# Per-token inverse rms, earlier key norms, paired low-rank products and moved second-half inputs in a hybrid decoder layer

## The chip, the cores and the metric

The kernel runs on one core of a Trainium2 chip. The metric is the device time of one execution in microseconds (us); lower is better. TensorE's granted clock is given as a share of full speed: 1.00 is 2.4 GHz, 0.50 is 1.2 GHz.

## The reference

One decoder layer on 512 tokens of width 1024, in float32:

```python
xn = x * rsqrt(mean(x*x) + 1e-6) * g_mix
z = xn @ w_in                          # 14 column tiles of 128 for RWKV, 8 for q and k, 512 columns of v
# RWKV-7 time mixing, 8 heads of 64, on z's first part (mixed with the previous token by mu)
decay = exp(-exp(-softplus(-(w0 + tanh(wd) @ w_up)) - 0.5))
a = sigmoid(a0 + ad @ a_up);  g = sigmoid(gd) @ g_up      # ranks 64, 64, 128
kk = k*k_k / max(norm_per_head(k*k_k), 1e-12);  k = k*(1 + (a-1)*k_a)
state = state*decay + (state @ -kk) (kk*a)^T + v k^T;  y = state @ r     # token by token
# dilated sliding-window attention, 8 heads of 64, rope on q and k
h = x + concat(groupnorm(y)+bonus, gated by g; attention) @ w_out
out = rms_norm(h + peer_ffn(rms_norm(h)))                 # product-key experts
```

## The kernel before

The program is a row of stages, and each engine runs its own written-out list of instructions; semaphores order them. The order is the order of the code. A stage ends for all engines together. The stages that the change touches take the first 330 us of 1735: `project`, `attend`, `prepare` and `scan`. The later ones (`finish`, `route`, `experts`) are not touched.

**`project`** multiplies x by w_in in 26 steps n. The operands are split in a high and a low part (`xn_hi`, `xn_lo`, `win_hi`, `win_lo`, type fp32r), and each product is three matmuls (`three_pass`, L203 to L205). Step n needs `win_hi` (ScalarE, L288) and `win_lo` (VectorE, L354). The normalization is applied afterwards: VectorE multiplies each result by `rstd`, the inverse rms of every token, spread over 128 partitions by 512 tokens (`take`, L323). ScalarE squares x (`sq`, in tile `qk`), TensorE sums the squares with a matrix of ones in the middle of step 1 (`squares`, L383), VectorE scales and takes the reciprocal (L307, L309), ScalarE the root (L294). VectorE's list then has `take(0)`, `take(1)` and only then `win_lo` of step 3. Before step 4, TensorE transposes `rstd` (L394) so that `x_rstd_col` has one token per partition; ScalarE uses it at the end for the four tiles of v (L299). At the start `NWARM` matmuls on zeros run while the first inputs load.

**`attend`** runs over i = 0 to 15 (4 head pairs by 4 query tiles). TensorE's list has `scores(i)` (L492, two 64-row matmuls for two heads), `turn(i-3)` (transposes, L501), `values` (L513, L528); VectorE takes the row maxima (L637) and scales (L650), ScalarE exponentiates (L587) and copies the turned tiles out (`take`, L596). At i = 16 TensorE sums the squares of the keys per head (`square_sums`, L547, 16 matmuls of 8 columns), and at i = 18 ScalarE takes the root of them (L619), which needs another function table.

**`prepare`** makes the inputs of the recurrence. Twelve low-rank products of 512 columns (`up`, L723: 0 to 3 decay, 4 to 7 a, 8 to 11 gate) and four that spread the inverse key norms (`spread`, L730) run on TensorE in the order 0-3, two spreads, 4-7, two spreads, 8-11. ScalarE takes the sigmoids in the order of the products (L751), VectorE the running sums (L780), `k_new` (L794), the normed keys (L784), and then the scaled inputs of the first half of the tokens (`scaled_half`, L672 to L688, in steps 0 to 5).

**`scan`** handles 8 chunks of 64 tokens, four per half. For chunks 0 to 3 TensorE multiplies the scaled inputs (all its matmuls here have line L933), VectorE masks the results (`take_b`, `take_k`, L1129). Then the triangular matrices are inverted in five levels (`inverses`, L1150, L1156). After each level of the first half VectorE does steps of `scaled_half` for the second half of the tokens, step 3 after the last. The chain over chunks (`chain`) starts when all of these (semaphore `s_late`) are done; GpSimd then multiplies `bonus` by `k_new` (L920).

## Time and profile before

| what | value |
|---|---|
| median of 3 runs | 1736.76 us (1733.96 to 1739.7) |
| the profiled execution | 1737.52 us, its span 1735.4 us |
| mean granted clock of TensorE | 0.983 |
| busy: PE, DVE, ACT, POOL | 1672.4, 1330.6, 700.9, 610.7 us |

PE is TensorE's matmuls, PEld its weight loads, DVE VectorE, ACT ScalarE, POOL GpSimd. Times in the profile count from the start of the span; the 2.1 us between time and span lie around it.
### The profile page before, as it was taken

Reading aid. Unit: us, or ns where it says so; the run is one execution under the profiler, and the core shown is the slowest. Engines: PE = TensorE matmul, PEld = TensorE weight load, DVE = VectorE, ACT = ScalarE, POOL = GpSimd, SP = SyncE. Lnnn points to the kernel's source line nnn. Section 1 sums busy time; section 2 is a strip of 40 time slices with the busy share of each in tenths; the row PEclk is TensorE's granted clock in tenths of the full one; section 3 lists DMA queues with packets and bytes.
Section 4 is the critical chain, followed back from the end, with each engine's and each line's share of the span. In section 5 each row is a group of like instructions: output and inputs, shape, how many; then the busy total and the mean of one; then the engine's idle time right before and its main releaser. Section 6 shows DMA issues by size and latency. Waiting matters only on the chain.

```text
span 1735.4 us, 29171 instructions
## 1 busy us (share of the span) xinstructions
PE 1672.4 (96%) x11401; PEld 1475.1 (85%) x11401; DVE 1330.6 (77%) x2732; ACT 700.9 (40%) x1080; POOL 610.7 (35%) x393
## 2 busy tenths in 40 slices
PE   9999989989899999999999999999999999999997
PEld 6877459968788888999999999999999998778886
DVE  5654755567399998999936668888888888888777
ACT  4111752224333334888853333333333333333334
POOL 0000110100256675333342236556565555443120
PEclk9999899999999999999999999999999999999999
DMA  6220010012223344455779788999999999999994
GB/s 237 87 96 25 1 50 4 4 55 105 79 97 116 116 150 156 164 215 204 269 270 343 242 288 323 366 348 349 349 351 359 355 335 323 396 371 365 326 313 177
DMA packets 128040, 380.88 MB, mean 219 GB/s; under 512 B 12064, under 2 KB 52384, under 8 KB 126880
## 3 DMA queue, kind: packets, MB, share of 16 engines
q1 hardware_dynamic: 81104, 207.28, 33.6%
q0 software_dynamic: 37728, 159.40, 24.8%
q10 hardware_dynamic: 9072, 12.35, 2.0%
q8 instruction: 90, 1.47, 0.3%
q14 instruction: 46, 0.38, 0.1%
HBM read 339.92 MB, written 39.06 MB: 218 GB/s over the span
## 4 chain that ended last, share of the span: by engine, by line
PE 46%; DVE 10%; DMA 2%; ACT 0%; issue 0%; POOL 0%; SPq 0%; DVEq 0%; ACTq 0%; POOLq 0%
PE ps L203 15%; PE ps L205 15%; PE ps L204 15%; DVE gated_cols L2116 5%; DVE wout_raw L2116 2%; DMA mixed<-hidden_ahead 2%; DVE wout_raw L2119 2%; PE ps L2234 1%; DVE v_lo L2169 0%; DVE h L2191 0%; ACT v_hi L2080 0%; DVE h L2198 0%; POOL u_lo L1976 0%; ACT u_selected L2041 0%; SPq L1924 0%
## 5 line engine op out<-in xcount | busy, mean ns | idle before, releaser
L203 PE MATMUL ps<-v_hi,a_hi 128*128 128x512 f32 x768 | 300.0, 391 | 4.6 <-DVE a_lo L2172 4.4
L204 PE MATMUL ps<-v_lo,a_hi 128*128 128x512 f32 x768 | 299.5, 390 | 0.0
L205 PE MATMUL ps<-v_hi,a_lo 128*128 128x512 f32 x768 | 299.5, 390 | 0.0
L1993 POOL DMA_INDIRECT v_selected<-in_v,expert_index x128 | 184.4, 1440 | 295.6 <-DVE h L2139 281.7
L203 PE MATMUL ps<-xn_hi,u_hi 128*128 128x384 f32 (+1 forms) x800 | 275.0, 344 | 10.6 <-DMA sub_keys<-in_keys_t 5.1
L204 PE MATMUL ps<-xn_lo,u_hi 128*128 128x384 f32 (+1 forms) x800 | 272.2, 340 | 0.0
L205 PE MATMUL ps<-xn_hi,u_lo 128*128 128x384 f32 (+1 forms) x800 | 272.1, 340 | 0.0
L2169 DVE TENSOR_TENSOR v_lo<-wout_raw,v_hi 128x1024 fp32r<-128x1024 f32 x128 | 156.7, 1224 | 100.6 <-ACT v_hi L2080 99.3
L1984 POOL DMA_INDIRECT u_selected<-in_u_rows,expert_index x128 | 180.2, 1407 | 138.7 <-DVE hidden_selected L2126 109.0
L2080 ACT ACTIVATE v_hi<-wout_raw 128x1024 fp32r<-128x1024 f32 x128 | 135.0, 1054 | 139.3 <-PE ps L205 139.3
L2073 ACT ACTIVATE hidden<-ps 128x384 f32<-128x384 f32 x68 | 33.4, 491 | 358.8 <-PE ps L205 358.8
L203 PEld LDWEIGHTS ps<-v_hi,a_hi 128*128 128x128 f32 x768 | 144.5, 188 | 35.0 <-DVE v_lo L2169 6.0
L205 PEld LDWEIGHTS ps<-v_hi,a_lo 128*128 128x128 f32 x768 | 144.6, 188 | 30.0
L1586 POOL TENSOR_TENSOR wq_lo<-wq_raw,wq_hi 128x1024 fp32r<-128x1024 f32 x44 | 113.0, 2569 | 157.8 <-ACT wq_hi L1633 157.8
L204 PEld LDWEIGHTS ps<-v_lo,a_hi 128*128 128x128 f32 x768 | 144.5, 188 | 27.3
L2139 DVE SCALAR_TENSOR_TENSOR h<-v_selected,act_selected,h 128x1024 f32<-128x1024 f32 x128 | 163.9, 1280 | 4.4 <-DMA v_selected<-in_v,expert_index 0.7
L203 PEld LDWEIGHTS ps<-xn_hi,u_hi 128*128 128x128 f32 x800 | 151.4, 189 | 15.0 <-DMA sub_keys<-in_keys_t 5.4
L2126 DVE CUSTOM_DVE_ANT_0 dot_products<-u_selected,xn_tok 128x1024 bf16<-128x1024 f32 x128 | 153.6, 1219 | 13.4 <-DMA u_selected<-in_u_rows,expert_index 13.3
L204 PEld LDWEIGHTS ps<-xn_lo,u_hi 128*128 128x128 f32 x800 | 151.4, 189 | 2.9
L205 PEld LDWEIGHTS ps<-xn_hi,u_lo 128*128 128x128 f32 x800 | 151.2, 189 | 0.6
L203 PE MATMUL ps<-xn_hi,wq_hi 128*128 128x384 f32 (+1 forms) x352 | 128.0, 364 | 6.6 <-POOL wq_lo L1586 6.5
L205 PE MATMUL ps<-xn_hi,wq_lo 128*128 128x384 f32 (+1 forms) x352 | 125.5, 356 | 0.0
(319 smaller groups left out, 3116.5 us busy)
## 6 DMA issues: line engine op xcount, KB each, us to landing
wq_raw<-in_u_t SPq DMA_DIRECT2D x128, 512.0 KB, 4.8
wout_raw<-in_v SPq DMA_DIRECT2D x128, 512.0 KB, 7.0
gate_matrix<-gate_stage POOLq DMA_DIRECT2D x6, 4096.0 KB, 14.3
gates<-gate_matrix SPq DMA_DIRECT2D x32, 768.0 KB, 8.2
win_raw<-in_win_t SPq DMA_DIRECT2D x25, 512.0 KB, 3.5
mixed<-hidden_ahead SPq DMA_DIRECT2D x60, 192.0 KB, 7.4
wq_raw<-in_wq_t SPq DMA_DIRECT2D x16, 512.0 KB, 3.9
hidden_ahead<-hidden_route ACTq DMA_DIRECT2D x30, 192.0 KB, 2.0
```

Source lines behind the costliest of these rows:

```text
L203: nc.tensor.matmul(out, w_hi, m_hi, start=first, stop=False)
L204: nc.tensor.matmul(out, w_hi, m_lo, start=False, stop=False)
L205: return nc.tensor.matmul(out, w_lo, m_hi, start=False, stop=last)
L1586: st.do(pool.tensor_tensor(w_lo[:, n % SPL, :], raw[:, n % RQ, :], w_hi[:, n % SPL, :].bitcast(F32), ALU.subtract), s_lo)
L1984: pool.indirect_dma_start(u_sel[:, i % GB, :], None, u_rows, bass.IndirectOffsetOnAxis(S.expert[:, i:i + 1], 0)).then_inc(s_usel[i % GB], 16)
L1993: pool.indirect_dma_start(v_sel[:, k % GB, :], None, v_rows, bass.IndirectOffsetOnAxis(S.expert[:, k:k + 1], 0)).then_inc(s_vsel[k % GB], 16)
L2080: act.activation(v_hi[:, n % 2, :], v_raw[:, n % VR, :], ACT.Copy).then_inc(s_vhi, 1)
L2116: v.tensor_scalar(cols[r % R][:, q, :], S.const("iota"), tab[:, 1, tok:tok + 1], tab[:, 2, tok:tok + 1], ALU.is_equal, ALU.mult).then_inc( ...
L2119: v.tensor_tensor(rows[r % R][:, :, :], bc(S.const("iota"), 1, Q), bc(tab[:, 0, r * Q:(r + 1) * Q], 2, NKEY), ALU.is_equal).then_inc(s_row ...
L2126: v.tensor_tensor_reduce(products[:, i % 2, :], u_sel[:, i % GB, :], S.xn_tok[:, :], 1.0, 0.0, ALU.mult, ALU.add, h_sel[:, i:i + 1]).then_ ...
L2139: v.scalar_tensor_tensor(S.h[:, GT, :], v_sel[:, k % GB, :], a_sel[:, k:k + 1], S.h[:, GT, :], ALU.mult, ALU.add).then_inc(s_sum, 1)
L2169: v.tensor_tensor(v_lo[:, p, :], v_raw[:, n % VR, :], v_hi[:, p, :].bitcast(F32), ALU.subtract).then_inc(s_vlo, 1)
```

## The change

- `project`: the sums of squares come out with one token per partition: 32 matmuls (4 token tiles by 8 tiles of x) whose weights are a 128x128 tile of the squares and whose moving operand is one column of ones. Scaling, reciprocal and root work on 128x4. VectorE then multiplies the identity by each token's value (`tmp`, 4 times 128x128), TensorE spreads that over all partitions with ones in the middle of step 2 (`spread`), and VectorE copies the result to `rstd`. The transposes before step 4 are gone. The last step signals after each token tile, so that ScalarE takes v tile by tile. `NWARM` goes from 24 to 15.
- `attend`: `square_sums` moves to i = 8 (bank 7), VectorE copies the sums out at i = 10, ScalarE takes the root at i = 16, right after the tanh.
- `prepare`: decay and a products alternate and use only their 64 rows of the contraction each (partitions 0 to 63, and 64 to 127); the spreads follow, then the gate products. ScalarE alternates too. VectorE does all running sums, all `k_new`, all normed keys.
- `scan`: steps 0, 1, 3 and 5 for the second half stand after the masks of chunks 0 to 3, steps 4 and 2 after levels 0 and 1. Step 3 is one instruction in place of four.

```diff
-                st.do(v.tensor_scalar(rstd[:, :], S.ps[:, 3, :], 1.0 / D, RMS_EPS, ALU.mult, ALU.add), s_mean)
-                st.settle()
-                st.do(v.reciprocal(rstd[:, :], rstd[:, :]), s_mean)
+                st.do(v.tensor_scalar(rstd_col[:, :], S.ps[:, 3, 0:TT], 1.0 / D, RMS_EPS, ALU.mult, ALU.add))
+                st.settle()
+                st.do(v.reciprocal(rstd_col[:, :], rstd_col[:, :]), s_mean)
+                dve.wait_ge(s_const, 48)
                 dve.wait_ge(s_rstd, 1)
+                for t in range(TT):
+                    st.do(v.tensor_scalar(tmp[:, 0, t * P:(t + 1) * P], S.const("ident"), rstd_col[:, t:t + 1], None,
+                                          ALU.mult), s_col)
+                dve.wait_ge(s_spread, 1)
+                st.do(v.tensor_copy(rstd[:, :], S.ps[:, 7, :]))
+                st.settle()
...
             def squares():
                 pe.wait_ge(s_const, 48)
-                for k in range(KT):
-                    pe.wait_ge(s_sq, k + 1)
-                    last = nc.tensor.matmul(S.ps[:, 3, :], S.const("ones"), sq[:, k, :], start=k == 0,
-                                            stop=k == KT - 1)
+                pe.wait_ge(s_sq, KT)
+                for t in range(TT):
+                    for k in range(KT):
+                        last = nc.tensor.matmul(S.ps[:, 3, t:t + 1], sq[:, k, t * P:(t + 1) * P],
+                                                S.const("ones")[:, 0:1], start=k == 0, stop=k == KT - 1)
                 last.then_inc(s_ms, 1)
+            def spread():
+                pe.wait_ge(s_col, TT)
+                for t in range(TT):
+                    last = nc.tensor.matmul(S.ps[:, 7, t * P:(t + 1) * P], S.const("ones"),
+                                            tmp[:, 0, t * P:(t + 1) * P], start=True, stop=True)
+                last.then_inc(s_spread, 1)
...
+                        if n == 2 and k == KT // 2:
+                            spread()
...
+                        if n == NWIN - 1:
+                            last.then_inc(s_vmm, 1)
...
                 if i == 2 * TT:
                     pe.wait_ge(s_vt, 8)
                     pe.wait_ge(s_vta, 8)
-                if i == NS:
                     square_sums()
+                if i == 3 * TT:
+                    pe.wait_ge(s_sum, 1)
...
                 if i == NS:
                     st.do(act.activation(WA[0:HD, :], WA[0:HD, :], ACT.Tanh))
-                if i == NS + 2:
-                    act.wait_ge(s_ssum, 1)
-                    st.do(act.activation(nrm[:, :], S.ps[:, 0, 0:TT * NHD], ACT.Sqrt), s_nrm)
+                    act.wait_ge(s_sum, 1)
+                    st.do(act.activation(nrm[:, :], nrm[:, :], ACT.Sqrt), s_nrm)
...
+            for j in range(HP):
+                w = slice(j * P, (j + 1) * P)
+                nc.tensor.matmul(S.ps[:, j, :], S.up[0:HD, 0, w], WA[0:HD, :], start=True, stop=True).then_inc(s_up, 1)
+                nc.tensor.matmul(S.ps[:, HP + j, :], S.up[HD:P, 1, w], WA[HD:P, :], start=True,
                                  stop=True).then_inc(s_up, 1)
...
-        for j in range(HP):
-            st.do(v.tensor_tensor(r_[:, j, :, :], R[:, j, x].rearrange("p (n t) -> p n t", t=C), after[:, j, :, :],
-                                  ALU.mult), signal)
+        st.do(v.tensor_tensor(r_, R[:, :, x].rearrange("p j (n t) -> p j n t", t=C), after, ALU.mult), signal)
...
-                        if not half and c == HC - 1:
-                            st.settle()
-                            for step in ((0,), (1, 5), (4,), (2,), (3,))[level]:
-                                scaled_half(S, dve, v, st, step, 1, s_late)
+                        if not half and c == HC - 1 and level < 2:
+                            other_half((4, 2)[level])
...
             for ch in range(HC):
                 take_b(ch)
                 take_k(ch)
+                other_half((0, 1, 3, 5)[ch])
```

On ACT at the end of `attend`, before (`probs_t<-ps` is `take`, `mixed<-ps` is `pair`, `z_mixed<-z_mixed` the tanh):

```order
L596 ACTIVATE probs_t<-ps 128x8x128
L616 ACTIVATE z_mixed<-z_mixed 64x512
L596 ACTIVATE probs_t<-ps 128x2x3x128
L603 ACTIVATE mixed<-ps 128x512
L596 ACTIVATE probs_t<-ps 128x2x2x128
L619 ACT_TABLE_LOAD
L619 ACTIVATE kk_norm<-ps 128x32
L596 ACTIVATE probs_t<-ps 128x2x128
```

The same place after the change:

```order
L608 ACTIVATE probs_t<-ps 128x8x128
L628 ACTIVATE z_mixed<-z_mixed 64x512
L630 ACT_TABLE_LOAD
L630 ACTIVATE kk_norm<-kk_norm 128x32
L608 ACTIVATE probs_t<-ps 128x2x3x128
L615 ACTIVATE mixed<-ps 128x512
L608 ACTIVATE probs_t<-ps 128x2x2x128
L608 ACTIVATE probs_t<-ps 128x2x128
```

The table load and the root now stand ahead of `take(13)` and `pair(1)`, where they stood behind `take(14)`.

On DVE in `scan`, from the last level's masks of the first half to the first chunk of the chain, before:

```order
L677 SCALAR_TENSOR_TENSOR r_and_a<-kk,decays 128x4x63 x4
L679 TENSOR_SCALAR r_and_a<-kk 128x4x4
L1150 TENSOR_TENSOR level_products<-ps,consts_scan 128x4x32 x4
L1156 TENSOR_TENSOR inverse_t<-inverse_t,ps 128x4x32 x4
L682 TENSOR_TENSOR r_and_a<-z_mixed,decays 128x4x64 x4
L684 COPY chunk_decay<-decays 128x4x4
L1177 TENSOR_TENSOR b_scaled<-ps,v_products 128x256
```

The same place after the change:

```order
L1143 TENSOR_TENSOR level_products<-ps,consts_scan 128x4x32 x4
L1149 TENSOR_TENSOR inverse_t<-inverse_t,ps 128x4x32 x4
L1168 TENSOR_TENSOR b_scaled<-ps,v_products 128x256
L1169 TENSOR_TENSOR b_scaled<-z_mixed,v_products 128x256
L1118 TENSOR_TENSOR inverse_t<-ps,consts_scan 128x256
```

Steps 2 and 3 of the second half (L677 to L684) are gone from in front of the chain.

## Rows read from the trace of the kernel before

**Rows 1.** The page: each engine's busy time, share and instructions.

```profile
PE 1672.4 (96%) x11401; PEld 1475.1 (85%) x11401; DVE 1330.6 (77%) x2732; ACT 700.9 (40%) x1080; POOL 610.7 (35%) x393
```

**Rows 2.** Timeline of `project`'s head: start us, us, instruction, idle before and releaser.

```profile
18.51 7.09 PE L383 MATMUL ps<-qk,consts 128*128 128x512 f32 x16
...
25.04 0.80 PE L203 MATMUL ps<-xn_hi,win_hi 128*128 128x512 f32 x1
...
30.42 0.69 DVE L323 TENSOR_TENSOR z_shift<-ps,x_rstd 128x512 f32<-128x512 f32 x1 [0.70 <-ACT x_rstd L294]
...
36.12 0.50 PE L203 MATMUL ps<-xn_hi,win_hi 128*128 128x512 f32 x1 [2.31 <-DVE win_lo L354]
...
43.34 0.60 PE L394 MATMUL ps<-consts_late,x_rstd 128*128 128x128 f32 x4
```

**Rows 3.** Timeline, PE: the key sums at `attend`'s end, 16 matmuls.

```profile
216.45 3.74 PE L547 MATMUL ps<-to_head_scaled,kk_square 128*128 128x8 f32 x32
```

**Rows 4.** Stretches: busy us and count of PE, PEld, DVE, ACT, POOL; granted clock; DMA.

```profile
37.38:40.79 3.41, 3.41 (x9) 2.64 (x8) 2.10 (x3) 0.00 (x0) 0.00 (x0) 0.50 0.48 154
197.80:201.20 3.40, 3.40 (x14) 1.65 (x10) 1.22 (x8) 1.31 (x6) 0.00 (x0) 0.50 0.00 0
216.45:220.05 3.60, 3.60 (x35) 3.60 (x33) 1.57 (x7) 1.88 (x5) 0.00 (x0) 1.00 0.00 0
...
301.47:307.00 5.53, 5.53 (x76) 5.53 (x78) 4.24 (x5) 0.38 (x1) 4.71 (x2) 0.50 0.01 3
309.13:315.54 6.41, 6.41 (x198) 6.41 (x196) 3.78 (x11) 1.97 (x7) 0.73 (x1) 1.00 0.02 5
```

**Rows 5.** Timeline: `project`'s end and `attend`'s first matmuls.

```profile
170.72 2.42 ACT L299 ACTIVATE v_tok<-ps,x_rstd_col 128x512 f32<-128x512 f32 x4 [16.12 <-PE ps L205]
...
173.45 0.49 PE L492 MATMUL ps<-qk 64*128 64x128 f32 x4 [2.81 <-PEq L211]
```

**Rows 6.** Timeline, PE in `attend`: after `scores(8)`, and a pair of 512 columns.

```profile
196.67 0.63 PE L501 MATMUL ps<-consts_late,scores 128*128 128x128 f32 x4 [0.57 <-DVE scores L650]
...
204.47 1.13 PE L492 MATMUL ps<-qk 64*128 64x512 f32 x4
```

**Rows 7.** Timeline of `attend`'s tail, ACT and PE.

```profile
217.72 0.61 ACT L616 ACTIVATE z_mixed<-z_mixed 64x512 f32<-64x512 f32 x1
220.94 0.81 ACT L596 ACTIVATE probs_t<-ps 128x768 f32<-128x768 f32 x1 [2.61 <-PE ps L501]
221.65 0.59 ACT L603 ACTIVATE mixed<-ps 128x512 f32<-128x512 f32 x1
...
224.71 1.28 ACT L619 ACT_TABLE_LOAD   x1
...
222.38 1.09 PE L528 MATMUL ps<-probs_t,v_tok 128*64 128x128 f32 x16 [0.47 <-ACT mixed L603]
```

**Rows 8.** Timeline of `prepare`: PE's products, DVE's wait for the third spread, step 0.

```profile
234.42 3.70 PE L723 MATMUL ps<-z_mixed,up_weights 128*128 128x512 f32 x8
...
239.21 0.75 DVE L784 SCALAR_TENSOR_TENSOR kk<-z_mixed,params,ps 128x512 f32<-128x512 f32 x1 [2.00 <-PE ps L730]
...
242.02 1.23 DVE L672 TENSOR_TENSOR k_new<-k_new,z_mixed 128x1024 f32<-128x1024 f32 x1
```

**Rows 9.** Timeline of `scan`: DVE before chunk 3's masks, and the start of the chain.

```profile
265.20 0.42 DVE L1129 TENSOR_TENSOR inverse_t<-ps,consts_scan 128x256 f32<-128x256 f32 x1 [2.45 <-PE ps L933]
...
299.49 0.29 DVE L1156 TENSOR_TENSOR inverse_t<-inverse_t,ps 128x128 f32<-128x128 f32 x1 [0.18 <-PE ps L933]
299.81 1.43 DVE L682 TENSOR_TENSOR r_and_a<-z_mixed,decays 128x256 f32<-128x256 f32 x4
...
301.41 4.52 POOL L920 TENSOR_TENSOR z_mixed<-z_mixed,k_new 128x2048 f32<-128x2048 f32 x1 [34.98 <-DVE chunk_decay L684]
...
301.47 0.80 PE L933 MATMUL ps<-z_mixed,r_and_a 64*64 64x64 f32 x10 [2.04 <-DVE chunk_decay L684]
...
303.07 3.13 DVE L1178 TENSOR_TENSOR b_scaled<-z_mixed,v_products 128x256 f32<-128x256 f32 x1
```

More of the change, by code:

```diff
@@ L390, in _ @@
             for n in range(NWIN):
-                if n == SPL + 1:
-                    pe.wait_ge(s_rstd, 1)
-                    for t in range(TT):
-                        last = nc.tensor.transpose(S.ps[:, 7, t * P:(t + 1) * P], rstd[:, t * P:(t + 1) * P],
-                                                   S.const("ident"))
-                    last.then_inc(s_col, 1)
                 pe.wait_ge(*((s_lo, n + 1) if n else (s_lo_half, 1)))
@@ L418, in _ @@
                                               w_hi[:, n % SPL, w], w_lo[:, n % SPL, w], k == 0, k == KT - 1)
-                last.then_inc(s_mm, 1)
+                        if n == NWIN - 1:
+                            last.then_inc(s_vmm, 1)
+                if n < NWIN - 1:
+                    last.then_inc(s_mm, 1)
                 if NRW < n < NRW + NQK + 1:
@@ L543, in square_sums @@
                 pe.wait_ge(s_ksq, 2 * HP)
-                pe.wait_ge(s_bias, 2 * NS)
                 for q in range(TT):
                     for j in range(HP):
-                        last = nc.tensor.matmul(S.ps[:, 0, q * NHD:(q + 1) * NHD], ksq[:, j, q * P:(q + 1) * P],
+                        last = nc.tensor.matmul(S.ps[:, 7, q * NHD:(q + 1) * NHD], ksq[:, j, q * P:(q + 1) * P],
                                                 to_head[:, j, :], start=j == 0, stop=j == HP - 1)
@@ L747, in _ @@
             st = Steps(act, S.own_act, S.counts)
-            def take_up(n, out, func, **kw):
-                act.wait_ge(s_up, n + 1)
-                st.do(act.activation(out, S.ps[:, up_bank(n), :], func, **kw), s_act)
             for j in range(HP):
-                take_up(j, sw[:, j, :], ACT.Sigmoid, bias=S.param("w0", j))
-            for j in range(HP):
-                take_up(HP + j, icl[:, j, :], ACT.Sigmoid, bias=S.param("a0", j))
+                act.wait_ge(s_up, 2 * j + 1)
+                st.do(act.activation(sw[:, j, :], S.ps[:, j, :], ACT.Sigmoid, bias=S.param("w0", j)), s_act)
+                act.wait_ge(s_up, 2 * j + 2)
+                st.do(act.activation(icl[:, j, :], S.ps[:, HP + j, :], ACT.Sigmoid, bias=S.param("a0", j)), s_act)
             st.do(act.activation(G, G, ACT.Sigmoid), s_gsig)
@@ L762, in _ @@
             for j in range(HP):
-                take_up(2 * HP + j, S.gate[:, j, :], ACT.Copy)
+                act.wait_ge(s_up, 2 * HP + j + 1)
+                st.do(act.activation(S.gate[:, j, :], S.ps[:, HP + j, :], ACT.Copy))
         @block.gpsimd
@@ L788, in _ @@
                 running_sum(j)
-                if j >= 2:
-                    normed_key(j - 2)
             dve.wait_ge(s_pd, 1)
             for j in range(HP):
-                dve.wait_ge(s_act, HP + j + 1)
+                dve.wait_ge(s_act, 2 * j + 2)
                 st.do(v.tensor_scalar(S.k_new[:, j, :], icl[:, j, :], S.param("k_a", j), omka[:, j:j + 1],
                                       ALU.mult, ALU.add))
-                if j < 2:
-                    normed_key(j + 2)
+            for j in range(HP):
+                normed_key(j)
             st.settle()
@@ L1142, in take_k, with other_half @@
                 masked(rkt[:, ch % 2], banks(ch)[1], 1, "inclusive", s_kev)
+            def other_half(step):
+                st.settle()
+                scaled_half(S, dve, v, st, step, 1, s_late)
             def inverses(half):
```

59 lines of the change are left out of this document (21 added, 38 removed).

## The prediction

> **What bounds the kernel now.** I read the page first: TensorE's matmuls are busy 96% of the span [rows 1]. So what counts is TensorE's idle time, its clock, and work that stands ahead of it on other engines. All edits lie in the first 330 us; what follows shifts with them as a whole, so the sum is made of what each edited place gains or loses on the path through TensorE. I then read the timelines of those places engine by engine, and the stretches with the granted clock. The reader is to see three things. In `project` TensorE stood 2.31 us because `win_lo` of step 3 is behind `take(0)` and `take(1)` on VectorE, and those are behind the inverse rms [rows 2]. In `scan` it stood 2.04 us behind step 3 of the second half [rows 9]. And after such pauses the clock fell to its lower level, 1.2 GHz, for some us: at 37.38 to 40.79, 197.80 to 201.20, 301.47 to 307.00 [rows 4]. A pause therefore costs itself and a second time afterwards.
>
> **The change part by part.** *Sums of squares.* Before, 16 passes of 512 columns ran from 18.51 to 25.04 [rows 2]: 6.5 us. After, 64 passes of one column, each with a load of 128x128 weights. The nearest row is the key sums: 32 passes of 8 columns in 3.74 us, 0.117 each, with the same weights [rows 3]. So 64 cost 7.5 us, and the sums end at 26.0, 1.0 us later than before. The bounds are 6.5 (no loss) and, with the clock at half, 15 (rival 3).
>
> The Trainium skill, page "TensorEngine Tiling (Array Packing)", section Performance Considerations, says that a matmul of one column takes as long as one of 60, about 60 cycles. By it the sums would cost an estimated 1.6 us instead of 7.5; this is rival 4. The key sums, also below 60 columns, took 0.117 us a pass, so the trace speaks against it where the weights change each time.
>
> *Chain to `take(0)`.* The scaling, reciprocal and root stood between 25.04 and 30.42 [rows 2]; on 128x4 instead of 128x512 they take a few tenths each. But the spreading stands behind the second half of step 1 and the first half of step 2 on TensorE, 24 matmuls. The 36 from 25.04 to the end of step 2 (36.12 - 2.31 = 33.8) took 8.8 us [rows 2], the first of them slow; I take 5.6 for 24. So `spread` starts at 31.6. By then the reciprocal, the root and four multiplications of the identity, together under 2 us after 26.0, are done by then: shortening them gains nothing. `spread` is 8 passes of 128 columns; the transposes, 4 such passes, hold 0.60 [rows 2], so about 0.9 us, and the copy of 128x512 costs 0.7 like L323. `take(0)` starts at 33.2 instead of 30.42: 2.8 us late. `take(1)`, `win_lo` of step 3 and TensorE's step 3 are queued behind it and come 2.8 late too. TensorE's pause before step 3 grows from 2.31 to about 4, but the clock is lost there before as well [rows 4]. The transposes' 0.4 goes. Net +2.4 (from +1.5 to +4).
>
> *Fewer warm-up matmuls*: nothing. Step 0 waits for x, and step 1 for its weights, which load in the time covered. If that cover were gone, the nine matmuls, 18 passes like those of the transposes (four in 0.60 [rows 2]), would be worth 2 us.
>
> *v tile by tile.* Four copies of 2.42 us stood between TensorE's last matmul and `attend` [rows 5]; three now lie under the matmuls of the other token tiles: -1.7. The pause of 2.81 shrinks to about 1.1.
>
> *Key sums in the middle.* TensorE works with hardly a gap from `scores(8)` on, so the 3.7 us push everything behind them, `turn(5)` first; they fill the 0.57 it waited there [rows 6]: +3.1. Right behind that pause the clock was 0.50 for 3.4 us [rows 4], which cost 1.7; with the pause filled it may be kept. I take the middle, +2.2 (from +1.4 to +3.1).
>
> *The tail of `attend`.* At i = 16 the sums are gone, 3.7 us. TensorE cannot use it all: ScalarE now has table load (1.28) and root (0.2) between the tanh, which ends at 218.3, and `take(13)` and `pair(1)` [rows 7]. These end at 218.3 + 1.5 + 0.7 + 0.6 = 221.1, and TensorE's `last_values`, which waited for that `pair`, starts at 221.2 instead of 222.38: -1.2. The late one is now ScalarE. TensorE pauses about 2.5 us before it, like the 2.31 that preceded the stretch at 37.38, so the clock may fall in the tail: up to +1.7 more, I take +0.8. Net -0.4. `attend` as a whole: +1.8 (from +0.2 to +3.6).
>
> *Products in twos.* Each product alone costs 0.9 (four in 3.70) [rows 8]. Two 64-row matmuls of 512 columns on different row halves, the scores of two heads, took 1.1 us together [rows 6], so they run side by side. The eight products take 4.3 us instead of 7.2. Now ScalarE sets the pace: eight sigmoids at 0.58 (the v copies, four in 2.42 with the last one's tail [rows 5]) end 4.6 us after its table load, and the third and fourth spreads no longer come behind eight products. VectorE waited 2.00 for the third spread [rows 8]; that goes. Its other work stays, but for step 3 of the first half in one instruction of 1.22 instead of four in 1.4: -0.2. It loses about 0.1 because each running sum now waits two sigmoids (1.16) and takes 1.12. Step 0 starts at about 240.0 instead of 242.02, and `scan` 2.3 earlier: net -2.3 (if the pairs don't run side by side -0.4).
>
> *Second-half inputs in the prelude.* VectorE stood idle before the masks of chunks 1, 2 and 3 alike, 2.45 us the last time [rows 9], and each step moved there costs 1.2 (like step 0 [rows 8]) to 1.4: hidden, and step 5 falls in the longer wait before the first level. Steps 4 and 2 stand behind levels 0 and 1, where such steps stood before. If the cover were gone, each would cost its 1.2 to 1.4. Step 3 stood on the path: the last addition ends at 299.78, TensorE could start 0.15 later, and started at 301.47 [rows 9]: -1.5. The first chunk of the chain took 7.66 (301.47 to 309.13) in the stretch at 0.50, the second 6.41 at 1.00 with 1.4 of extra products [rows 4]; at full clock it is 5.0. With the pause at about 0.5 the clock is likely kept: 2.7, times two thirds: -1.8. GpSimd's product of 4.52 us ran beside VectorE's L1178, which took 3.13 where the next ones take 0.4 [rows 9]; TensorE had work all that time, so this cost nothing. It now runs in the levels, where VectorE's operations read PSUM, and L1177 beside it was not slowed. Net -3.3 (from 0 to -4.2).
>
> **Sum.** +2.4 - 1.7 + 1.8 - 2.3 - 3.3 = -3.1 us. The profiled execution took 1737.52 (span 1735.4 and 2.1 around it), which gives 1734.4; it stood 0.8 above the median of the runs shown, so the median becomes 1736.76 - 3.1 = 1733.7.
>
> **Rivals.** *1. The clock is kept at every place.* The middle of `attend` costs 1.4, its tail -1.2, and `scan` gives -4.2: 2.4 - 1.7 + 0.2 - 2.3 - 4.2 = -5.6, 1731.2. For it: three pauses shrink [rows 5, 6, 9]. Against: two new ones of 2.5 and 4 us appear. Chance 0.2.
>
> *2. The gains are eaten.* The pairs don't overlap (-0.4), the clock falls in `attend`'s tail (+3.6 for the stage) and again in `scan` (-1.5): 2.4 - 1.7 + 3.6 - 0.4 - 1.5 = +2.4; with one or two of the three, about 0, 1737. For it: the clock fell after each pause of 2 us. Against: the scores' pair. Chance 0.22.
>
> *3. The one-column passes cost the clock, and the kernel is slower.* TensorE does nothing but weight loads for 7.5 us. The key sums, 3.7 us long, ran at full clock [rows 4], but no row shows a stretch twice as long. If it falls after 2 us, 48 passes cost 0.23 instead of 0.117, +5.6, and the 24 matmuls behind run partly at 0.43: +1.7 to +3.4. All of it lies in front of `spread` and so of `take(0)`. Sum -3.1 + 8.2 = +5.1: 1741.9. It decides against the change from a loss of 3.1 on, and is measurable from 8.3. Chance 0.12.
>
> *4. One-column passes are nearly free*, because the weight loads hide. The cheapest passes of the trace are those of the chain, 198 in 6.41 us, 0.032 each [rows 4], on tiles of a quarter of the size. By that the 64 cost 2.1 instead of 7.5, and `take(0)` starts 5.4 earlier: -3.1 - 5.4 = -8.5, 1728.3. Against it stands the row of the key sums. Chance 0.03.
>
> **How the numbers follow.** The forecast of about -3 has 0.43. A difference under 0.3% (5.2 us) is what a measurement of this kernel can't tell from none. Faster by more: most of rival 1, rival 4 and the forecast's edge, 0.26. Slower by more: half of rival 3 and rival 2's edge, 0.08. Within: 0.66. The range reaches from beyond rival 1 to short of rival 3: 1728 to 1740.5. Cases of both signs hold chance, but the likeliest alone spans 1731.5 to 1736.
>
> **What would show it.** In the profile after: the squares as 64 passes in about 7.5 us at clock 1.00; L331 (`take(0)`) at about 33; TensorE's pause before step 3 near 4 us, released by `win_lo`; about 1.1 us between TensorE's last product of `project` and the first scores; the key sums for 3.7 us behind `scores(8)`; ScalarE's table load right behind the tanh and a pause of TensorE of 2.5 us before `last_values`; eight products in about 4.3 us, VectorE without a 2 us wait in `prepare`; no wait on the chunk decay before the chain, and no operation of 3 us behind it. Wrong would make it above all a different clock in one of these places, a spread that doesn't wait in TensorE's order, or a stage behind 330 us that doesn't shift along.

## The result, and the profile after

The changed kernel takes 1750.42 us (median of five, 1747.6 to 1753.64) against 1736.76 before: the ratio is 1.0071, 95% interval 1.0056 to 1.0087, so it is slower by 9.7 to 15.1 us. The forecast was 1733.7 with a range of 1728 to 1740.5. The profiled execution took 1747.78 us, its span 1745.7. These are five executions of each kernel; two single later ones of the changed kernel, in other groups of runs, took 1746.89 where the kernel before had a median of 1738.16 (1.0050), and 1742.95 where it had 1737.76 (1.0030). Both lie below the interval, so prices that are taken below as differences from 1.0071 may be too high.

I profiled both kernels three times. Each column below is one profiled execution, in us; the pieces are cut at starts of TensorE's or VectorE's instructions, so they add up to the span.

| piece | before | after | mean difference | forecast |
|---|---|---|---|---|
| start to step 3 of `project` | 36.1, 35.1, 35.3 | 42.9, 44.2, 42.2 | +7.6 | +2.8 |
| step 3 to the first scores | 137.3, 135.7, 137.3 | 135.0, 136.3, 135.0 | -1.4 | -2.1 (v -1.7, transposes -0.4) |
| `attend` | 55.5, 56.4, 55.3 | 61.0, 61.4, 60.7 | +5.3 | +1.8 |
| `prepare` | 21.1, 21.1, 21.1 | 19.0, 19.0, 19.0 | -2.1 | -2.3 |
| `scan` to the product with the first chunk's decay | 58.4, 57.5, 58.2 | 53.2, 53.5, 53.1 | -4.7 | -3.3 |
| from there to the first product with wq (rest of `scan`, `finish`, head of `route`) | 148.6, 151.1, 148.0 | 147.7, 147.9, 147.6 | -1.5 | 0 |
| from there to the end | 1278.4, 1279.1, 1280.9 | 1286.9, 1282.9, 1283.4 | +4.9 | 0 |

So the three profiles are 8.1 us apart in the mean, less than the 13.7 between the medians of the timed runs. Against the forecast the head of `project` lost 4.8 us more, `attend` 3.5 more, and the last row 4.9, where nothing is changed.

The timeline of TensorE in `project` after, which answers to [rows 2]:

```profile
17.42 0.39 PE L205 MATMUL ps<-xn_hi,win_lo 128*128 128x512 f32 x1
17.78 9.24 PE L388 MATMUL ps<-consts,qk 128*128 128x1 f32 x64
26.88 0.77 PE L203 MATMUL ps<-xn_hi,win_hi 128*128 128x512 f32 x1
27.45 0.63 PE L204 MATMUL ps<-xn_lo,win_hi 128*128 128x512 f32 x1
...
42.85 0.50 PE L203 MATMUL ps<-xn_hi,win_hi 128*128 128x512 f32 x1 [3.72 <-DVE win_lo L362]
```

VectorE behind it, the same stretch:

```profile
36.41 0.69 DVE L317 COPY x_rstd<-ps 128x512 f32<-128x512 f32 x1 [7.76 <-PE ps L396]
37.14 0.69 DVE L331 TENSOR_TENSOR z_shift<-ps,x_rstd 128x512 f32<-128x512 f32 x1
...
41.58 1.22 DVE L362 TENSOR_TENSOR win_lo<-win_raw,win_hi 128x1024 fp32r<-128x1024 f32 x1
```

The stretches of the changed kernel with busy times and the granted clock (the figure of 0.50 to 1.00 under PEclk, behind the five busy times), the squares in two pieces, the products behind them, and the key sums of `attend`; they answer to [rows 4]:

```profile
core 0: us, PE busy (x) PEld busy (x) DVE busy (x) ACT busy (x) POOL busy (x), PEclk, DMA share, GB/s
17.78:22.80 5.02, 5.02 (x46) 5.02 (x46) 1.22 (x1) 2.34 (x2) 0.00 (x0) 1.00 1.03 412
22.80:26.88 4.08, 4.08 (x21) 4.08 (x21) 0.00 (x0) 0.00 (x0) 0.00 (x0) 0.50 0.71 285
26.88:33.00 6.12, 6.12 (x15) 4.77 (x16) 1.21 (x6) 1.71 (x3) 0.00 (x0) 0.50 0.00 1
199.36:205.40 6.04, 6.04 (x33) 6.04 (x33) 1.76 (x10) 2.39 (x9) 0.00 (x0) 0.58 0.01 3
```

Read the pieces by pass: about 45 passes in 5.02 us are 0.112 each at 1.00; the rest take 4.08 us, 0.213 each, at 0.50. TensorE is never idle here, and the clock still drops to 1.2 GHz in the middle of the sums and stays there for 6 us of the products of steps 1 and 2. The key sums take 6.04 instead of 3.6 from start to start (216.45 to 220.05 in [rows 4]), at a mean clock of 0.58:

```profile
198.33 1.10 PE L504 MATMUL ps<-qk 64*128 64x128 f32 x4 [0.88 <-DVE row_max L648]
199.36 6.19 PE L558 MATMUL ps<-to_head_scaled,kk_square 128*128 128x8 f32 x32
```

The gains came nearly as forecast or above. The copies of v now lie under the matmuls, the last one alone behind them (to [rows 5]); the pairs run side by side, one pair in 0.43 us (to [rows 8]); the pause before the chain fell from 2.04 to 0.39 and the clock stays at 1.00 behind it (to [rows 9]):

```profile
174.14 0.69 ACT L300 ACTIVATE v_tok<-ps,x_rstd_col 128x512 f32<-128x512 f32 x1 [0.59 <-PE ps L205]
175.50 0.69 ACT L300 ACTIVATE v_tok<-ps,x_rstd_col 128x512 f32<-128x512 f32 x1 [0.67 <-PE ps L205]
176.86 0.69 ACT L300 ACTIVATE v_tok<-ps,x_rstd_col 128x512 f32<-128x512 f32 x1 [0.67 <-PE ps L205]
```

```profile
239.76 0.59 PE L727 MATMUL ps<-z_mixed,up_weights 64*128 64x512 f32 x1
239.80 0.59 PE L728 MATMUL ps<-z_mixed,up_weights 64*128 64x512 f32 x1
240.19 0.59 PE L727 MATMUL ps<-z_mixed,up_weights 64*128 64x512 f32 x1
...
306.74 1.15 PE L922 MATMUL ps<-z_mixed,r_and_a 64*64 64x64 f32 x32 [0.39 <-DVE inverse_t L1149]
```

```profile
300.00:306.70 6.70, 6.35 (x218) 6.24 (x214) 3.05 (x11) 1.11 (x4) 0.00 (x0) 1.00 0.02 5
306.70:311.10 4.40, 4.36 (x120) 4.36 (x122) 2.30 (x7) 0.38 (x1) 0.73 (x1) 1.00 0.02 4
```

In `attend`'s tail ScalarE's list stands as forecast, and TensorE's pause before `last_values` is the 2.5 us that I named (to [rows 7]). A stretch at 0.50 of 3.4 us follows from 231.0 on:

```profile
227.25 0.61 ACT L628 ACTIVATE z_mixed<-z_mixed 64x512 f32<-64x512 f32 x1
227.88 1.28 ACT L630 ACT_TABLE_LOAD   x1
229.18 0.23 ACT L630 ACTIVATE kk_norm<-kk_norm 128x32 f32<-128x32 f32 x1
...
230.74 1.78 PE L540 MATMUL ps<-probs_t,v_tok 128*64 128x128 f32 x16 [2.49 <-ACT mixed L615]
```

The last row of the table is a surprise of another kind: nothing is changed there. The chain of the changed kernel shows one place of it, and VectorE's timeline the wait:

```profile
908.60 12.50 DMA gates<-gate_matrix
921.10 0.03 issue
921.15 0.04 issue
921.19 0.56 DVE hidden L2157
921.75 1.15 DVE v_lo L2161
```

```profile
921.19 0.56 DVE L2157 TENSOR_TENSOR hidden<-hidden,gates 128x384 f32<-128x384 f32 x1 [3.04 <-DMA gates<-gate_matrix]
921.67 1.22 DVE L2161 TENSOR_TENSOR v_lo<-wout_raw,v_hi 128x1024 fp32r<-128x1024 f32 x1
```

In this chain the first load of the gates in `experts` takes 12.5 us. In the kernel before it took 7.55 (904.60 to 912.15), and VectorE did not wait for it. TensorE's first product with `v_hi` waits 2.32 us for this.

### The profile page after: what moved, and what is told of

The parts are those of the page before. It is cut to its first block, busy times and chain, and to the rows that moved or that the text cites. A ratio compares the mean times of both kernels' runs of the same rounds, so it can differ in the third digit from the quotient of the medians.

```text
span 1745.7 us, 29239 instructions
## 1 busy us (share of the span) xinstructions
PE 1675.7 (96%) x11435; PEld 1482.3 (85%) x11435; DVE 1317.3 (75%) x2731; ACT 699.9 (40%) x1080; POOL 611.5 (35%) x393
## 4 chain that ended last, share of the span: by engine, by line
PE 50%; DVE 5%; DMA 4%; issue 1%; ACT 0%; POOL 0%; SPq 0%; DVEq 0%; ACTq 0%; POOLq 0%
PE ps L203 16%; PE ps L204 15%; PE ps L205 15%; PE ps L2226 4%; DMA mixed<-hidden_ahead 3%; DVE gated_cols L2108 1%; DVE wout_raw L2108 1%; DMA gates<-gate_matrix 1%; DVE wout_raw L2111 1%; DVE v_lo L2161 1%; DVE h L2131 0%; DVE h L2183 0%; ACT v_hi L2072 0%; DVE a_lo L2164 0%; DVE dot_products L2118 0%
## 5 line engine op out<-in xcount | busy, mean ns | idle before, releaser
L2131 DVE SCALAR_TENSOR_TENSOR h<-v_selected,act_selected,h 128x1024 f32<-128x1024 f32 x128 | 163.9, 1280 | 4.7 <-DMA v_selected<-in_v,expert_index 1.0
L204 PE MATMUL ps<-xn_lo,wq_hi 128*128 128x384 f32 (+1 forms) x352 | 126.2, 359 | 0.0
```

Of the source, the lines that this page charges most:

```text
L204: nc.tensor.matmul(out, w_hi, m_lo, start=False, stop=False)
L2131: v.scalar_tensor_tensor(S.h[:, GT, :], v_sel[:, k % GB, :], a_sel[:, k:k + 1], S.h[:, GT, :], ALU.mult, ALU.add).then_inc(s_sum, 1)
```

## The experiments

Theory A: sums on TensorE with few columns per pass make the clock fall, and that costs the two new sums their forecast. Rival B: the later stages lose when their start moves. Rival C: the sums cost only the forecast and something else is late. Ratios are to the kernel before, timed on the same chip; the changed kernel itself was timed in one group of runs only, so a difference from its 1.0071 compares two groups.

**Undoing one part, or taking one alone.** `e1_old_rms` is the changed kernel with `project`'s inverse rms put back, with the transposes and 24 warm-up matmuls that belong to it. The cut shows the sums alone:

```diff
-                        last = nc.tensor.matmul(S.ps[:, 3, t:t + 1], sq[:, k, t * P:(t + 1) * P],
-                                                S.const("ones")[:, 0:1], start=k == 0, stop=k == KT - 1)
+                    last = nc.tensor.matmul(S.ps[:, 3, :], S.const("ones"), sq[:, k, :], start=k == 0,
+                                            stop=k == KT - 1)
```

> The changed kernel with only the inverse rms of project put back (512-column sums, transposes, 24 warm-up matmuls); everything else as changed. Theory A (the 64 one-column passes cost TensorE its clock and are the largest loss): step 3 starts near 36.1 again instead of 42.9, the stretch at the lower clock from 22.8 to 33.0 is gone, and the time falls by about 6.5 us, to 1744 (ratio to before about 1.004). Rival B (the loss arises mostly in the later, untouched stages, which answer badly to any displaced start): the first 60 us gain 6 us but the end gains at most 2, 1748 to 1750. Rival C (the squares cost only what was forecast, 2.4, and the rest of the loss in project is something else): 1748.

Measured: 0.9992 [0.9982, 1.0001]; step 3 starts at 34.4, no stretch at 0.50 before 35. The edit of the squares, with its spreading and its warm-ups, was worth 0.79% in the changed kernel, about 13.7 us, twice theory A's 6.5. Of these the profile shows 8.4 at step 3 and 6.8 at the first product with wq.

`e2_old_attend` is the changed kernel with the key sums back at i = 16 and ScalarE's root at i = 18 (TensorE's lines):

```diff
+                if i == NS:
                     square_sums()
-                if i == 3 * TT:
-                    pe.wait_ge(s_sum, 1)
```

> The changed kernel with the key norms of attend put back (sums at i = 16, root at i = 18); everything else as changed. Theory A (the key sums behind a short pause lose the clock: 6.2 us instead of 3.7 and slow matmuls behind them): attend takes 3.5 us less than in the changed kernel (it lost 5.5 there: from +4.4 at its start to +9.9 at its end), the time is about 1746 (ratio 1.005). Rival B (later stages answer to a displaced start): the end doesn't follow, 1750. Rival C (the middle would be slow anyway, clock falling there with the old order too): attend gains only 1 to 2 us, 1748.5.

Measured: 0.9998 [0.9985, 1.0011], again more than the 3.5 us of theory A: 0.73%. `attend` takes 54.5 us instead of 61.0. Rival C of this run, that the stage would be nearly as slow in the old order, falls: `attend` is 6.5 us shorter. The squares of this run show the clock at its clearest, here 17.00 to 19.60 and then the whole low stretch:

```profile
17.00:19.60 2.60, 2.60 (x25) 2.60 (x25) 0.64 (x1) 1.71 (x2) 0.00 (x0) 0.99 1.04 421
19.60:33.30 13.70, 13.70 (x54) 12.58 (x54) 1.80 (x7) 1.78 (x3) 0.00 (x0) 0.50 0.43 170
```

13.7 us at half clock without a gap; so the loss in `project` isn't the same in each execution. Step 3 started at 42.9, 44.2, 42.2 and 43.6 in four profiles with these sums.

`e3_good` is the kernel before with the three edits without small sums, of which the cut shows one line each; `e4_rms_only` is the kernel before with the first item of the change but for the copies of v, 15 warm-up matmuls included:

```diff
+                act.wait_ge(s_vmm, t + 1)
...
+                nc.tensor.matmul(S.ps[:, HP + j, :], S.up[HD:P, 1, w], WA[HD:P, :], start=True,
...
+                other_half((0, 1, 3, 5)[ch])
```

> Before with three of the five edits: v tile by tile, products in twos, second-half inputs in the prelude. The two edits with small key or token sums on TensorE are left as before. Theory A: the three are worth 1.7 + 2.1 + 5.1 = 8.9 us by the marks of the changed kernel's trace, and nothing is lost: 1728 (ratio 0.995). Rival B (later stages lose about 7.5 us whenever the start of finish moves): 1735.5, about the same as before, with extra stretches at the lower clock behind 600 us. Rival C (the scan's gain of 5.1 is partly an accident of the clock; the forecast 3.3 holds): 1729.5.

> Before with the inverse rms alone (one-column sums, spread by the identity, 15 warm-up matmuls). Theory A: one-column sums take about 9 us with the clock at 0.50 from their middle on, step 3 starts 6.7 us later, and the time is 1743 (ratio 1.0036). Rival B (later stages answer to the displaced start): 1750, nearly all of the changed kernel's loss from this edit alone. Rival C (as forecast, +2.4): 1739.

Measured: `e3_good` 0.9962 [0.995, 0.9974], faster than before by 4.5 to 8.7 us, about what the three forecasts add up to (-7.3), less than theory A's 8.9; in its profile the first product with wq stood 10.7 us ahead of the mean of before's three, and from there to the end it took 1285.1 us, 5.6 more than their mean. So the late loss comes without any small sum too. `e4_rms_only` 1.0056 [1.0033, 1.0079], 9.7 us slower where A said 6; step 3 at 40.3, the clock low from 22.2 to 29.0 and again from 39.2 on. C (+2.4) falls.

`f4_keys_only` is the kernel before with the key norms' move alone (TensorE's lines).

```diff
-                if i == NS:
                     square_sums()
+                if i == 3 * TT:
+                    pe.wait_ge(s_sum, 1)
```

> Before with the key norms' move alone (8 columns per pass, i = 8). Removing it from the changed kernel gave 0.73%, adding it to the version with three edits only 0.30%. Theory A (its cost in attend is the same everywhere, 5.5 to 6 us there, and what is beyond that is the late part's): attend takes 61 us instead of 55.5, ratio 1.003 to 1.004. Rival (it costs its 12 us only together with other edits): attend 57 to 58, ratio 1.001. Rival B of the late part (every program other than before loses 4 to 5 us there): ratio 1.006.

Measured: 1.0038 [1.0024, 1.0052], 6.6 us, within A's range. `attend` took 58.9 in its profile, 3.1 more than before's mean and short of A's 61; the key sums were at 0.50 from 196.2 on, for 6.8 us. This execution also shows what a clock stretch costs elsewhere: the levels and the start of the chain ran at 0.50 for 20.5 us, and the piece from `scan`'s start to the first decay took 65.2 instead of 58.

```profile
295.10:315.60 20.50, 18.48 (x323) 18.37 (x321) 10.47 (x27) 1.54 (x6) 4.70 (x2) 0.50 0.01 2
```

**Changing only the width of the small sums.** This is the experiment that tests theory A's cause. The same 64 passes with the same weights stream 128 columns of ones instead of one, and VectorE reads one column of each 128; the second kernel does the same to the key sums (8 heads' weights repeated 16 times). The cuts show TensorE's lines; the edits of what VectorE reads and of the tile `to_head_scaled` are left out.

```diff
-                        last = nc.tensor.matmul(S.ps[:, 3, t:t + 1], sq[:, k, t * P:(t + 1) * P],
-                                                S.const("ones")[:, 0:1], start=k == 0, stop=k == KT - 1)
+                        last = nc.tensor.matmul(S.ps[:, 3, t * P:(t + 1) * P], sq[:, k, t * P:(t + 1) * P],
+                                                S.const("ones")[:, 0:P], start=k == 0, stop=k == KT - 1)
```

> The changed kernel with the sums of squares of project streaming 128 columns of ones per pass instead of one; the same 64 passes with the same weights, and VectorE reads one column of each 128. Theory A (weight loads with hardly a column behind them let the clock fall; the load sets the price of a pass): a pass still costs 0.112 us, the clock stays at 1.00, the sums take 7.2 us instead of 9.1 and the matmuls behind them run at full clock: step 3 starts near 38.5 to 39 instead of 42.9 and the time falls by 4 us, to 1746.5 (ratio 1.005). Rival B (the clock falls for a reason other than the width, such as the load on the chip of the passes themselves): the low stretch stays at 22.8, nothing gained, 1750.5. Rival C (a pass costs more with 128 columns): 0.2 us a pass, 13 us, slower, 1755.

```diff
-                        last = nc.tensor.matmul(S.ps[:, 7, q * NHD:(q + 1) * NHD], ksq[:, j, q * P:(q + 1) * P],
+                        last = nc.tensor.matmul(S.ps[:, 7, q * P:(q + 1) * P], ksq[:, j, q * P:(q + 1) * P],
```

> As the run before this one (128 columns of ones), and the key sums of attend also stream 128 columns (16 repetitions of the 8 heads' weights) instead of 8, in the same 32 passes at the same place. Theory A: the low stretch around 200.3 (10.2 us long) goes or shrinks to 3.4, the key sums take 3.7 instead of 6.2 us, attend takes 57 to 58 us instead of 61.0, and the time falls by another 3 us, to 1743.5 (ratio 1.003). Rival B (there it is the pause before the sums that costs the clock, not their width): attend stays at 61, no difference to the run before. Rival C: wider passes cost more, attend 62 or more.

Measured: `e6_wide_ones` 1.0015 [1.0003, 1.0028], `e7_wide_both` 0.9974 [0.9958, 0.999]. The second step, -0.41% or 7.1 us, was timed on one chip. The first is -0.56%, 9.7 us, from the changed kernel's 1.0071, another group of runs; in the profiles the first product with wq comes 5.4 us earlier than in the mean of the changed kernel's three. Both are for streaming more columns. With both sums wide the same change is faster than the kernel before, by 0.10 to 0.42%, 1.7 to 7.3 us. The squares of `e6_wide_ones` in its timeline:

```profile
17.11 7.38 PE L388 MATMUL ps<-consts,qk 128*128 128x128 f32 x64
24.25 0.48 PE L203 MATMUL ps<-xn_hi,win_hi 128*128 128x512 f32 x1
24.57 0.39 PE L204 MATMUL ps<-xn_lo,win_hi 128*128 128x512 f32 x1
```

And the stretches of `e7_wide_both`, the squares and the key sums:

```profile
16.80:23.90 7.10, 7.10 (x64) 7.10 (x64) 1.22 (x1) 2.34 (x2) 0.00 (x0) 1.00 1.03 411
192.41:196.08 3.67, 3.67 (x33) 3.67 (x33) 1.76 (x10) 2.39 (x9) 0.00 (x0) 1.00 0.02 4
```

A pass costs 0.111 us with 128 columns as with one. The clock is 1.00 in both sums, and step 3 starts at 37.3 and 37.0. The key sums take 3.67 us here although the same pause of 0.88 us stands before them:

```profile
191.38 1.10 PE L504 MATMUL ps<-qk 64*128 64x128 f32 x4 [0.88 <-DVE row_max L648]
192.41 3.84 PE L558 MATMUL ps<-to_head_scaled,kk_square 128*128 128x128 f32 x32
196.08 0.60 PE L513 MATMUL ps<-consts_late,scores 128*128 128x128 f32 x4
```

`attend` takes 53.8 us in `e7_wide_both` and 61.3 in `e6_wide_ones`, whose key sums are still narrow. For the first 310 us the rivals B and C of these runs fall; at the key sums the next version narrows what may be said.

**A version from these findings.** `e11_best` keeps the old squares and has all else, with wide key sums. Its edit is that of `e1_old_rms` together with the second one above, so against `e1_old_rms` it differs in the width of the key sums alone.

> A version from the findings: the sums of squares of project as before, everything else as changed, but the key sums of attend with 128 columns per pass. Theory A (narrow sums cost the clock; wide ones are cheap): attend takes 54 us, as where both were wide, project starts step 3 near 34.4, wq starts near 443 to 444.5, 1 to 2 us earlier than in the run with three edits, and the time is 1730 (ratio 0.995). Rival (key sums in the middle gain nothing over those at the end): the same as with three edits, ratio 0.9962. If the old sums of project leave attend in another state of the clock: attend 57 or more, ratio 0.998.

Measured: 0.9955 [0.9938, 0.9972], 1732.41 us: the fastest, ahead of before by 0.28 to 0.62%, but not to be told from `e3_good`. Moving the key norms gains nothing then that can be measured. `attend` took 56.8, not 54, and the clock was low from 190.7 on, inside the wide key sums, behind the same pause of 0.88:

```profile
189.77:195.07 5.30, 5.30 (x33) 5.30 (x33) 1.76 (x10) 2.39 (x9) 0.00 (x0) 0.68 0.00 0
190.70:194.10 3.40, 3.40 (x19) 3.40 (x18) 0.83 (x3) 1.46 (x7) 0.00 (x0) 0.50 0.00 0
```

So 128 columns don't always keep the clock in that place. What the profiles do show is the length: with 8 columns the clock was low there in six of six profiles, for 6.8 to 10.2 us and `attend` took 58.9 to 61.4; with 128 columns it was low in one of two, for 3.4 us, and `attend` took 53.8 and 56.8. In timed runs the width gave 0.41% (`e7_wide_both` against `e6_wide_ones`) and 0.37% (`e11_best` against `e1_old_rms`, on two chips).

**The later stages.** `e5_before_again`, `f1_before_third`, `e12_after_again` and `f3_after_third` are the two kernels unchanged; `e8_before_delayed` and `e9_before_wide_warm` (profiled again as `f2_wide_warm_again`) delay everything, the first by more warm-up instructions, the second by wider ones; `e10_before_few_warm` has fewer, wider ones and no delay. The cuts leave out that VectorE clears the wider operand of zeros.

```diff
-        NWARM = 24
+        NWARM = 64
```

```diff
-                nc.tensor.matmul(S.ps[:, 7, 0:P], zd[:, 0, 0:P], zd[:, 0, 0:P], start=True, stop=True)
+                nc.tensor.matmul(S.ps[:, 7, 0:364], zd[:, 0, 0:P], zd[:, 0, 0:364], start=True, stop=True)
```

```diff
-        NWARM = 24
+        NWARM = 15
-                nc.tensor.matmul(S.ps[:, 7, 0:P], zd[:, 0, 0:P], zd[:, 0, 0:P], start=True, stop=True)
+                nc.tensor.matmul(S.ps[:, 7, 0:218], zd[:, 0, 0:P], zd[:, 0, 0:218], start=True, stop=True)
```

> The kernel before, unchanged, profiled a second time. From the start of the product with wq (457.0 us) to the end took 1278.4 us in the first profile of before, and 1282 to 1287 in the five profiles of other versions, though nothing is changed there. Theory A (the later stages vary from run to run by a few us, and the first profile of before was a lucky one): this second one takes 1281 to 1284 there. Rival B (the later stages answer to the moved start): again 1278 to 1279.

> The kernel before with 64 warm-up matmuls instead of 24: nothing but a later start of everything, by about 4 to 5 us (80 more passes at 0.11 to 0.15, part of them under the loads of the first inputs). Theory A (the stages shift as a whole): the end moves by what step 3 of project moves, within 1 us; between the start of wq and the end it takes 1281 to 1284 as in the other versions. Rival B (the later stages answer to a displaced start with 5 to 8 us of their own): the end moves by 10 us or more where step 3 moves by 4 to 5. Rival C (the delay is absorbed by loads that arrive anyway): the time stays within 2 us of before.

> The kernel before with the same 24 warm-up matmuls, each 364 instead of 128 columns wide: the same number of instructions, but everything starts about as late as with 64 warm-ups (step 0 near 17.6 us). From the start of wq to the end took 1278.4 and 1279.1 us in the two profiles of before and 1282 to 1287 in all eight others, with 64 warm-ups 1285. Theory A (the later stages answer to the moved start): here also 1283 to 1286, the first load of gates takes 12 us instead of 7.6, and the end is 13 us later than before's profile. Rival B (they answer to the instructions' number, which shifts how the program itself is loaded): 1278 to 1279, the end about 7 us later.

> The kernel before with 15 warm-up matmuls, as in the change, but 218 columns wide: 9 instructions of TensorE fewer, at about the same times. Theory A (the later stages answer to the moved start): from wq to the end 1278 to 1279 as in before, time unchanged within 1.5 us. Rival B (they answer to the number of instructions ahead of them): 1282 to 1285 from wq to the end, and the time 3 to 6 us longer, though no stage starts later.

> The changed kernel, unchanged, profiled a second time. Its first profile lost 2.4 us in route (waits of TensorE on GpSimd's wq_lo and a clock fall at 654) and 6.3 us behind it against before. Theory A (both come with this program every time): from the start of wq to the end again 1286 to 1288 and the low stretch at 22.8 again. Rival (the part in route is chance): 1283 to 1285, as in the other versions.

> The kernel before, unchanged, a third profile. From the start of wq to the end it took 1278.4 and 1279.1 us, in the two profiles of the changed kernel 1286.9 and 1282.9. Theory A (the short late part belongs to this program): 1278 to 1280, no pause of TensorE before its first product with v_hi. Rival B (chance, drawn anew in every execution): anything from 1278 to 1287, a pause of 2 to 4 us there in two of three executions.

> Before with 24 warm-up matmuls of 364 columns, a second profile. The first took 1742.2 us in all, the lowest of six executions whose median was 1749.0. Theory A (the late part belongs to the program): wq to the end again 1280 to 1281, and the rest of the difference to the median lies in the first 460 us. Rival B (chance in every execution): it is 1284 to 1287 this time, with the pause before v_hi.

> The changed kernel, unchanged, a third profile. Theory A (the late part belongs to the program): 1283 to 1287 from wq to the end, the pause of 2 to 3 us before v_hi again, and the one-column sums at the lower clock from 19.5 to 23 us on again. Rival B (chance in every execution): in one of three cases no pause there and 1279 to 1281.

| kernel | ratio | step 3 | wq to the end | TensorE waits before `v_hi` |
|---|---|---|---|---|
| before, three times | 1 | 36.1, 35.1, 35.3 | 1278.4, 1279.1, 1280.9 | no, no, no |
| 15 warm-ups, 218 columns | 0.9996 [0.9985, 1.0008] | 35.3 | 1281.0 | no |
| 24 warm-ups, 364 columns, twice | 1.0058 [1.004, 1.0076] | 44.4, 45.0 | 1280.4, 1282.3 | no, no |
| 64 warm-ups | 1.0041 [1.0027, 1.0055] | 43.4 | 1285.2 | yes |
| changed, three times | 1.0071 [1.0056, 1.0087] | 42.9, 44.2, 42.2 | 1286.9, 1282.9, 1283.4 | yes, yes, yes |

Several expectations of these runs missed: from wq to the end the second profile of before took 1279.1 (A: 1281 to 1284), the second of the changed kernel 1282.9 (A: 1286 to 1288, its rival 1283 to 1285), and the wide warm-ups 1280.4 without the wait, where A had 1283 to 1286 with it. The third profiles took 1280.9 without the wait (A: 1278 to 1280) and 1283.4 with it (A: 1283 to 1287).

Two things follow. A pure delay comes out at the end about one to one: 7.9 us at step 3 against 0.41%, 7.1 us, and 9.2 us against 0.58%, 10.1. (The profiled execution with 64 warm-ups was the longest of six, 1749.4.) So there is no 5 to 8 us penalty for a moved start as such; rival B is not borne out by these timed runs. And the wait before `v_hi` came with the program in all that were profiled more than once: never in six profiles of before and of two of its variants, in each of three of the changed kernel. It also stands in the single profile of each other version (1.5 to 2.9 us), `e3_good` among them, and these took 1281.2 to 1285.4 from wq to the end. VectorE stands for the load of the gates just ahead of it. The kernel before:

```profile
L1930 SPq DMA_DIRECT2D gates<-gate_matrix x2: 376/382/387, 904.6 to 914.9; - x2
DMA to landing us min/median/max: 4.7/6.2/7.6
```

The changed kernel, its second profile:

```profile
L1922 SPq DMA_DIRECT2D gates<-gate_matrix x2: 377/396/414, 910.5 to 922.1; - x2
its engine sat idle before it (us, times) until:
  DMA gates<-gate_matrix: 3.0, 1
DMA to landing us min/median/max: 6.3/9.2/12.1
```

The first of two such loads took 7.6 against 12.1 us. Where its landing is on record it took 7.6, 7.5 and 10.2 us in three profiles without the wait, and 11.7 to 12.7 in six with it; the other two profiles of before have no landing for it, only no wait. Why it lands later in this program is open. Neither the number of instructions ahead (15 and 64 warm-ups differ in the wait, 24 and 15 don't) nor the delay (24 wide ones: none) decides it alone. Nor was it shown what the rest of the later loss is: the wait is worth some 2 of the 4.9 us; in the first profile of the changed kernel waits on GpSimd and a low stretch in `route` added 3, which the other two lack (wq to the end 1282.9 and 1283.4), so that part differs between executions of one program.

## Why the prediction was wrong

- **Sums of squares.** This step failed. I took 7.5 us, with "the clock at half, 15" as the far bound and rival 3 at a chance of 0.12. The price per pass was right (0.112 for 0.117, which counted the last pass to its end), the clock was not: it fell 2.0 to 5.3 us into the sums in five profiles. They took 9.1 us (up to 11.8 in another profile), the 24 matmuls to `spread` 8.4 instead of 5.6, `take(0)` came at 37.1 instead of 33.2, and step 3 7.6 us later than before instead of 2.8. Rival 3's mechanism is what happened, at about half its size: it had +8.2 on top of the forecast, and the three profiles show +4.8 at step 3. With 128 columns the sums took 7.1 and step 3 came 1.7 us late (2.8 forecast, with step 1 begun some 0.9 earlier), so the chain behind the sums was sound and the clock was the term that failed.
- **Key sums in the middle.** This step failed too. The term was +2.2 with an upper bound of 3.1, from sums of 3.7 us at full clock as they ran at the end; `attend` as a whole was to give +1.8 and gave +5.3. The sums took 6.0 us, with 10.2 us at 0.50 from just behind their start. The pause of 0.57 was filled, as I meant it to be; another of 0.88 stands ahead of `scores(8)` in the kernel before and after alike. Filling the pause didn't keep the clock, and the term had no fall inside the sums. Eight columns alone don't bring the fall, for at the end of `attend` they kept the clock; in the middle, 128 columns shortened or removed the stretch.
- **The tail of `attend`** went as told: table load, root, a pause of 2.49, a stretch at 0.50.
- **v tile by tile, products in twos:** -1.4 (with the transposes) and -2.1 for -2.1 and -2.3. Right in mechanism; the pause before `attend` fell from 2.81 to 1.03, as forecast.
- **Second-half inputs:** -4.7 for -3.3; the clock was kept whole, the case that I had put at two thirds. Its bound was -4.2, so the gain lies beyond the range of this term, and by what isn't located.
- **Fewer warm-up matmuls:** not measured apart; step 0 started 1.6 us earlier, step 1 0.9, and the late `take(0)` swallows both.
- **"What follows shifts with them as a whole"** failed too: +4.9 us arise behind the first product with wq in the mean of the profiles. About 2 are the wait for the gates, the rest isn't located. It comes with the three edits without small sums as well.
- **Their sum.** The edits' timed prices don't add up simply: the three good ones -0.38%, the squares +0.56% alone and +0.79% within the changed kernel, the key norms +0.38% alone and +0.73% within. Against `e3_good` each of the two small sums costs 0.36% and 0.30%, and the changed kernel has both and 0.4% more. In wq's start there is no such remainder between these four versions: squares +6.6 and +6.8 by two pairs (`e2_old_attend` against `e3_good`, changed against `e1_old_rms`). Alone against before's mean the two stand at +1.8 and +9.5 there, single profiles with other low stretches. The remainder is either in the later part or in the 1.0071 itself, which two later executions didn't reach; this stays open.
- **What the forecast was worth with the clock kept.** With both sums wide the change gives -0.26% [-0.42, -0.10], 4.5 us faster, around the forecast's -3.1. The late loss is in that figure as well, so the near agreement is partly luck.

The Trainium skill, page "TensorE: Matmul & The Clock Gate", section LDWEIGHTS, says that loading P columns of weights takes about P/1.2 ns, an estimated 107 ns for 128. The rows at full clock agree: 0.112 us a pass for 1 and for 128 streamed columns. The rule of rival 4 (the Trainium skill, page "TensorEngine Tiling (Array Packing)", Performance Considerations) gives a matmul of one column about 60 cycles. No row here with a new 128x128 load in each pass came near that.

## What to carry to other kernels

A sum on TensorE with one to eight columns per pass may have to be priced twice: the passes, and the clock of the sum and of what stands behind it. As long as a pass costs the same, try more columns, even useless ones; here 128 columns cost no more than one (0.111 us), and gave back 0.4% of the kernel at the key sums and, less firmly, 0.3 to 0.6% at the squares. Price a clock fall not at the small matmuls but at the long ones behind them and at whoever waits for these. And add edits one by one: three of five here were worth 0.38%, two undid it.

## What the runs showed that I had not expected

- The clock falls in the midst of unbroken work: with 64 one-column passes at 22.8, 19.6, 19.5, 21.6 and 22.2 us, in five of five profiles, 2.0 to 5.3 us into the sums; never with 128 or 512 columns in the same place (thirteen of thirteen). The length at 0.50 varied from 6.8 to 13.7 us.
- The same kernel's low stretches vary elsewhere as well: a second profile of before has one of 10.2 us in the middle of the chain that the first lacks:

```profile
355.10:365.30 10.20, 9.82 (x164) 8.91 (x162) 3.15 (x8) 2.61 (x6) 0.00 (x0) 0.50 0.01 2
```

- One load of 768 KB took 7.6 us in one program and about 12 in others; VectorE waited for it in all three profiles of the changed kernel and in none of the kernel before.
